# Rotary halves swapped by transfers inside SBUF instead of by matrix products, in a one-layer hybrid attention kernel

## What is computed

```python
def _rope(x, cos, sin):
    x1, x2 = jnp.split(x, 2, axis=-1)
    return jnp.concatenate([x1 * cos - x2 * sin, x2 * cos + x1 * sin], axis=-1)
```

## Time and profile before

| | |
|---|---|
| median of 3 runs | 2755.79 us |
| profiled execution | 2759.88 us |
| its span on the core | 2758.1 us, granted TensorE clock 0.972 |
| TensorE busy | 91% |
| VectorE busy | 63% |
| ScalarE busy | 51% |
| GpSimd busy | 15% |

### The profile page before, as it was taken

How to read it: one execution, slowest core, us unless ns; L and a number is a source line. 1 busy time by engine, 2 the same in 40 slices (tenths; PEclk the granted TensorE clock), 3 DMA queues, 4 the chain that set the end, 5 groups by cost and what they waited for, 6 DMA issues and landing times.

```text
span 2758.1 us, 36858 instructions
## 1 busy us (share of the span) xinstructions
PE 2501.3 (91%) x12861; PEld 2076.0 (75%) x12861; DVE 1749.0 (63%) x3573; ACT 1395.1 (51%) x2817; POOL 410.6 (15%) x397
## 2 busy tenths in 40 slices
PE   5998999998899999998889999999988889888997
PEld 5776888776778888887767788888666677777776
DVE  6467666224667677226777878732578888776652
ACT  5455655343656444224656645523466674545541
POOL 5334253441010000100010010010000000000010
PEclk8999999999999999999999999999999999999999
DMA  5757585794443422565243331146423324211125
GB/s 170 227 170 223 166 274 169 230 295 149 160 159 130 160 93 69 181 223 181 89 158 108 132 120 47 54 163 226 171 96 122 115 87 164 71 54 47 61 89 187
DMA packets 172583, 399.32 MB, mean 145 GB/s; under 512 B 13808, under 2 KB 96752, under 8 KB 162416
## 3 DMA queue, kind: packets, MB, share of 16 engines
q1 hardware_dynamic: 172400, 396.96, 43.2%
HBM read 308.31 MB, written 88.60 MB: 144 GB/s over the span
## 4 chain that ended last, share of the span: by engine, by line
PE 53%; DVE 19%; ACT 16%; issue 10%; DMA 1%; POOL 1%; SPq 0%; DVEq 0%; ACTq 0%; POOLq 0%
PE bank L893 38%; PE TR L789 5%; PE PV L860 5%; ACT signs L1058 4%; ACT prob L1023 3%; ACT prob L1033 3%; ACT ptH L1047 2%; DVE nmx L1427 2%; DVE score L1675 2%; DVE ptL L1458 2%; PE bank L800 2%; PE bank L801 2%; DVE prob L1417 2%; DVE zs L1493 1%; ACT squared L1002 1%
## 5 line engine op out<-in xcount | busy, mean ns | idle before, releaser
L893 PE MATMUL bank<-hH,pairs 128*128 128x512 f32 (+1 forms) x3584 | 1157.6, 393 | 18.1 <-DVE zs L1525 7.6
L893 PEld LDWEIGHTS bank<-hH,pairs 128*128 128x128 f32 x3584 | 678.5, 191 | 156.7 <-issue 18.7
L893 PE MATMUL bank<-hL,pairs 128*128 128x512 f32 (+2 forms) x1792 | 703.4, 393 | 0.0
L1058 ACT ACTIVATE signs<-score,bits 128x384 int8<-128x384 f32 (+7 forms) x256 | 335.8, 1312 | 214.4 <-DVE bits L1558 201.3
L1458 DVE TENSOR_TENSOR ptL<-TR,ptH 128x512 fp32r<-128x512 f32 (+1 forms) x384 | 257.0, 671 | 283.0 <-ACT ptH L1047 280.1
L893 PEld LDWEIGHTS bank<-hL,pairs 128*128 128x128 f32 (+1 forms) x1792 | 343.2, 192 | 64.6
L1047 ACT ACTIVATE ptH<-TR 128x512 fp32r<-128x512 f32 (+1 forms) x384 | 219.5, 576 | 319.5 <-PE TR L789 318.6
L1539 DVE TENSOR_SCALAR_CACHE_REDUCE above<-score,bits 128x256 uint8<-128x256 f32 (+8 forms) x264 | 326.5, 1237 | 9.4
L789 PE MATMUL TR<-identR,prob 128*128 128x128 f32 x1480 | 233.3, 279 | 84.9 <-ACT prob L1033 51.3
L789 PEld LDWEIGHTS TR<-identR,prob 128*128 128x128 f32 x1480 | 180.0, 142 | 158.2 <-ACT prob L1033 65.0
L893 PE MATMUL bank<-ysH,pairs 128*128 128x512 f32 x768 | 257.2, 397 | 10.6 <-issue 5.8
(11 more groups left out here) (215 smaller groups left out, 3648.9 us busy)
## 6 DMA issues: line engine op xcount, KB each, us to landing
pairs<-w_split SPq DMA_DIRECT2D x444, 512.0 KB, 3.5
w_split<-pairs SPq DMA_DIRECT2D x74, 1024.0 KB, 5.0
raw<-in_w_in SPq DMA_DIRECT2D x106, 256.0 KB, 5.6
xs<-in_x SPq DMA_DIRECT2D x4, 2048.0 KB, 9.3
rows<-in_x SPq DMA_DIRECT2D x16, 512.0 KB, 5.0
table<-trig SPq DMA_DIRECT2D x48, 128.0 KB, 3.0
raw<-in_w_branch SPq DMA_DIRECT2D x24, 256.0 KB, 5.8
out<-rows SPq DMA_DIRECT2D x3, 2048.0 KB, 7.5
```

Of the source, the lines that this page charges most:

```text
L893: done = nc.tensor.matmul(PJ[st.u + half * up][0:min(st.width, P), 0:st.n_tok], lhs, rhs[:, row, 0:st.n_tok], start=(n % 12 == 0 and (up o ...
L1058: nc.scalar.activation(signs[:, 0:keys], score[:, tt, 0:keys], ACT.Sign, bias=thr.bitcast(F32)[:, tt:tt + 1], scale=-1.0, accum_out=cnt[:, ...
```

## The change

The halves are swapped by transfers: behind each unit ScalarE issues one transfer per quarter of 32 partitions (four for a unit of 128 channels, two for 64) from `fT` into the new buffer `swapped`. The products L924 and L925, the copy into `fH`, the subtraction into `fL` and `swapR` go. The sign moves into the table: alternate quarters load the sines negated, from a table that is twice as wide. `rotated` adds `swapped` from SBUF instead of `TR` from PSUM. The core of the diff:

```diff
                 if st.role in ROPED:
-                    swaps.append(take("tr"))
-                    steps.append(Step("rope", unit=st, k=st.k, tr=swaps[-1], first=(st is units[0])))
-                    if st.role in ("kv", "kiw"):
-                        f_freed.pop()
-                    f_freed.append(("tr_full", swaps[-1] + 1))
+                    steps.append(Step("rope", unit=st, k=st.k, first=(st is units[0])))
+                    if st.role not in ("kv", "kiw"):
+                        f_freed.append([])
+                    n_swaps[st.k % 2] += 2 if st.role in ("kv", "kiw") else 4
+                    st.swapped = 16 * n_swaps[st.k % 2]
+                    f_freed[-1].append((f"swapped{st.k % 2}", st.swapped))
...
+        def swap_halves(queue, un):
+
+            queue.wait_ge(S["f_sin"], un.k + 1)
+            if un.k >= 2:
+                queue.wait_ge(S["f_sum"], un.k - 1)
+            for q in range(rows_of(un).stop // 32):
+                other = q + 1 - 2 * (q % 2)
+                queue.dma_start(swapped[32 * q:32 * q + 32, un.k % 2, :],
+                                staged(un)[32 * other:32 * other + 32, :]).then_inc(S[f"swapped{un.k % 2}"], 16)
...
-                    sp.wait_ge(S["sin_ready"], 2)
-                    for i, of in enumerate((1, 0)):
-                        sp.dma_start(trig.rearrange("g f n -> (g f) n")[:, i * T:(i + 1) * T], folded[of][:, :]).then_inc(S["tables_out"], 16)
+                    sp.wait_ge(S["sin_ready"], 3)
+                    for i, of in enumerate((folded[1], folded[0], folded[1], turns)):
+                        sp.dma_start(trig.rearrange("g f n -> (g f) n")[:, i * T:(i + 1) * T], of[:, :]).then_inc(S["tables_out"], 16)
...
-                elif st.kind == "rope":
-                    lanes = rows_of(st.unit)
-                    pe.wait_ge(S["tr_free"], st.tr - 1)
-                    pe.wait_ge(S["f_lo"], st.k + 1)
-                    bank = TR[st.tr % 2][lanes, :]
-                    nc.tensor.matmul(bank, swapR[lanes, lanes], fH[lanes, :], start=True, stop=False)
-                    nc.tensor.matmul(bank, swapR[lanes, lanes], fL[lanes, :], start=False, stop=True).then_inc(S["tr_full"], 1)
...
-                    act.wait_ge(S["f_sin"], st.k + 1)
-                    if st.k:
-                        act.wait_ge(S["tr_full"], swaps[st.k - 1] + 1)
-                    nc.scalar.activation(fH[lanes, :], staged(st)[lanes, :], ACT.Copy).then_inc(S["f_hi"], 1)
+                    swap_halves(act, st)
...
+                    act.wait_ge(S["sin_ready"], 2)
+                    nc.scalar.activation(turns[:, :], folded[0][:, :], ACT.Copy, scale=-1.0).then_inc(S["sin_ready"], 1)
...
-                    act.wait_ge(S["tr_free"], st.tr + 1)
+                    act.wait_ge(S["f_sum"], st.k + 1)
...
-                if st.role in ROPED and last == PRODUCTS:
-                    lanes, f = rows_of(st), staged(st)
-                    pool.wait_ge(S["f_hi"], st.k + 1)
-                    nc.gpsimd.tensor_tensor(fL[lanes, :], f[lanes, :], fH[lanes, :].bitcast(F32), ALU.subtract).then_inc(S["f_lo"], 1)
...
-                dve.wait_ge(S["tr_full"], st.tr + 1)
+                dve.wait_ge(S[f"swapped{st.k % 2}"], st.unit.swapped)
                 dve.wait_ge(S["dve_pj"], st.unit.used)
-                TT(turn[lanes, st.k % 4, :], TR[st.tr % 2][lanes, :], turn[lanes, st.k % 4, :], ALU.add).then_inc(S["tr_free"], 1)
+                TT(turn[lanes, st.k % 4, :], swapped[lanes, st.k % 2, :], turn[lanes, st.k % 4, :], ALU.add).then_inc(S["f_sum"], 1)
```

More of the change, by code:

```diff
@@ L73, in __init__ @@
         self.tr, self.p, self.pv, self.before, self.slots, self.behind = tr, p, pv, before, slots, behind
-        self.tiles, self.kept, self.gates, self.stored = tiles, kept, None, None
+        self.tiles, self.kept, self.gates, self.stored, self.swapped = tiles, kept, None, None, None
         self.scale, self.norm, self.woven, self.ring, self.read = scale, norm, woven, ring, read
@@ L86, in order_of_work @@
     count = dict(act_pj=0, dve_pj=0, act_s=0, dve_s=0, pool_x=0)
-    pj_freed, s_freed, x_freed, f_freed, swaps = [], [], [], [], []
+    pj_freed, s_freed, x_freed, f_freed, n_swaps = [], [], [], [], [0, 0]
     last_out, last_gates, places_of = None, [], {}
@@ L179, in turned @@
                 if st.role in ROPED:
-                    steps.append(Step("halve", unit=st, k=st.k, tr=swaps[-1]))
+                    steps.append(Step("halve", unit=st, k=st.k))
         if finishing is not None:
@@ L407, in order_of_work @@
     finish_last(NG - 1)
-    return steps, every, pj_bank, s_bank, s_freed, x_freed, f_freed, swaps
+    return steps, every, pj_bank, s_bank, s_freed, x_freed, f_freed
 def hybrid_block(nc, x, mem, positions, g_in, w_in, attn_sinks, g_mem, w_mem_kv, w_branch, w_out,
                  g_final, out):
-    steps, units, pj_bank, s_bank, s_freed, x_freed, f_freed, swaps = order_of_work()
+    steps, units, pj_bank, s_bank, s_freed, x_freed, f_freed = order_of_work()
     x_v = x[0].rearrange("(g t p) d -> g p t d", t=NT, p=P)
@@ L421, in hybrid_block @@
     mem_scratch = nc.dram_tensor("mem_scratch", (P, 4096), F32, kind="Internal").ap()
-    trig = nc.dram_tensor("trig", (NG, HD // 2, 2 * T), F32, kind="Internal").ap()
+    trig = nc.dram_tensor("trig", (NG, HD // 2, 4 * T), F32, kind="Internal").ap()
     once = sum(st.src == "w_mem_kv" for st in units)
@@ L495, in hybrid_block @@
         fT = sb("fT", [P, 2, T], offset=p_at)
-        fH, fL = (sb(name, [P, T], F32R, p_at + 4096 + i * 2048) for i, name in enumerate(("fH", "fL")))
+        swapped = sb("swapped", [P, 2, T], offset=p_at + 4096)
         turn = sb("turn", [P, 4, T], offset=p_at + 8192)
@@ L523, in hybrid_block @@
         wmask = sb("wmask", [P, 2, 256], F32R)
-        identR, swapR = sb("identR", [P, P], F32R), sb("swapR", [P, P], F32R)
+        identR = sb("identR", [P, P], F32R)
         wi = sb("wi", [P, NT, 4])
@@ L640, in hybrid_block @@
         block = ctx.enter_context(nc.Block())
-        freed_by = {n: S[n] for n in ("act_pj", "dve_pj", "act_s", "dve_s", "p_exp", "pool_x", "tr_full")}
+        freed_by = {n: S[n] for n in ("act_pj", "dve_pj", "act_s", "dve_s", "p_exp", "pool_x", "tr_full", "swapped0", "swapped1")}
         def blocks_of(tile, un):
@@ L663, in gate_of @@
             return kept[:, st.m, :] if st.kept else sg[:, st.x % 2, :]
+        def swap_halves(queue, un):
[6 more added lines that the diff above has]
+                                staged(un)[32 * other:32 * other + 32, :]).then_inc(S[f"swapped{un.k % 2}"], 16)
         def wait_free(eng, ring, index):
             if index >= 2:
-                engine, value = ring[index - 2]
-                eng.wait_ge(freed_by[engine], value)
+                for engine, value in ring[index - 2] if type(ring[index - 2]) is list else [ring[index - 2]]:
+                    eng.wait_ge(freed_by[engine], value)
         def wait_bank(of_kind, index):
@@ L750, in _ @@
                         rows_at = slice(32 * quarter, 32 * quarter + 32)
-                        sp.dma_start(table[rows_at, :, :].rearrange("p a n -> p (a n)"), trig[st.g]).then_inc(S["tables_in"], 16)
+                        sp.dma_start(table[rows_at, :, :].rearrange("p a n -> p (a n)"),
+                                     trig[st.g, :, quarter % 2 * 2 * T:(quarter % 2 + 1) * 2 * T]).then_inc(S["tables_in"], 16)
                 elif st.kind == "unit":
@@ L1282, in _ @@
             pool.wait_ge(S["consts"], 1)
-            link(nc.gpsimd.memset(made[:, :], 0.0))
-            for q in range(4):
-                to, other = made[:, 32 * q:32 * q + 32], 32 * q + (-32 if q % 2 else 32)
-                link(nc.gpsimd.affine_select(out=to, in_=to, compare_op=ALU.not_equal, fill=1.0 if q % 2 else -1.0,
-                                             base=-other, pattern=[[-1, 32]], channel_multiplier=1))
-            link(nc.gpsimd.tensor_copy(swapR[:, :], made[:, :]))
             link(nc.gpsimd.memset(wmask[:, :, :].bitcast(F32), 0.0))
```

7 lines of the change are left out of this document (3 added, 4 removed).

## The result

The changed kernel takes **2782.0 us** (median of 4 runs, 2778.9 to 2784.7), against 2755.6 for the kernel before on the same chip: a ratio of 1.009 (95% interval 1.0074 to 1.0106). It is slower by 26 us by the medians, where the forecast was 27 us faster; the time lies 30 us over the range and close to rival A's 2785. The profiled execution took 2781.2 us, 21.3 us of span more than before.

What follows compares the result with a forecast made beforehand. Pace was set by TensorE in most sparse stages, VectorE in group 3's, and a VectorE-ScalarE ring in window stages. Terms summed to -27.1 us: profiled 2759.9 to 2732.8, median 2729; range 2713 to 2752.

Steps and rivals of the forecast that it cites:

- rival A: Four issues cost ScalarE 3.83 us and it becomes the bound; decides from about 3 us; +29, 2785 us, chance 0.11.
- Step 2: ScalarE drops a 0.63 us copy and issues four transfers for 1.72 us, taken from SyncE's table loads; bounds nothing and 3.83.
- step 3: First stages, groups 1 to 3: fT starts 7.81 us apart for 8.92; 3.1 us gained a stage, 9.2 for three.
- Step 4: Window stages: 2.9 us gained a stage, 8.7 for groups 1 to 3; 2.0 in group 0 (bounds 0 and 6).
- hold-up of 0.76: Window stages: GpSimd's fL delays a small VectorE step by 0.76 us for three q; the change would remove this.
- (a): Window q rounds: issues end at 822.42, signs wanted at 822.37, so ScalarE is 0.05 us late and 0.7 is left.
- (b): Window ak: issues end at 785.2, landing adds 2.2 to 3.0 us; 0.8 us counted of the 1.05 possible.
- Step 1: 104 products removed: 5.5 us gained in group 0's first stage and groups 1 and 2's sparse stages, 0.9 in group 0's sparse.
- Step 5: Sparse stage of group 3, bound by VectorE: two hold-ups by GpSimd go, 1.5 us gained.
- Step 6: Elsewhere: transfers have the next projection, 5.5 us, to land; start costs +0.7; table stores nothing; group 0 may lose 1 us a unit.
- B: Group 0: ScalarE's issues wait for SyncE's on a shared issue path, 0.6 us a unit, +8, 2737 us, chance 0.12.
- C: First stages give nothing as another wait replaces the one for TR, nor does ak: 12 us lost, 2741 us, chance 0.17.

Runs made afterwards that it cites:

- e2: Changed kernel with all transfers still issued, but VectorE adds unswapped fT without waiting for their landing (wrong sum): 2764.2 us, 1.0019 of the kernel before.
- e1: Changed kernel without the swap: no transfers, VectorE adds unswapped fT (wrong sum), products and copies stay out: 2729.4 us, 0.9901 of the kernel before.
- e14: Repeat of e1, the changed kernel without transfers, run beside e13 on the same chip: 2732.2 us, 0.9907 of the kernel before.
- e12: Changed kernel with products in group 0 and for ak, and SyncE issuing the other transfers in groups 1 to 3: 2730.4 us, 0.9904 of the kernel before.
- e9: Changed kernel with the four ak units back on copy, fL and products, ScalarE issuing for the other 48: 2769.8 us, 1.0047 of the kernel before.
- e11: Changed kernel with products in group 0 and SyncE issuing all transfers in groups 1 to 3, ak included: 2733.0 us, 0.9912 of the kernel before.
- e10: Kernel before, all 52 units by products, with only the table of signed sines and a matrix of ones added: 2758.8 us, 1.0003 of the kernel before.
- e7: Changed kernel with SyncE in place of ScalarE issuing the same transfers for all units: 2764.5 us, 1.0033 of the kernel before.
- e3: Changed kernel with one issue a unit for the same bytes, halves copied and not swapped (wrong sum): 2742.9 us, 0.9936 of the kernel before.
- e8: Changed kernel with each transfer cut in two by columns, eight issues a unit on ScalarE, same bytes: 2878.7 us, 1.0437 of the kernel before.
- e13: As e1, but in group 0 VectorE's sum takes its second operand from PSUM (wrong sum): 2731.3 us, 0.9897 of the kernel before.
- e4: Changed kernel with GpSimd in place of ScalarE issuing the same four transfers: 2764.3 us, 1.0018 of the kernel before.

## Why the prediction was wrong, step by step

**Step 2, the price of four issues: right kind, wrong size.** I took 1.72 us from the table loads; it is 2.44. My break-even of 3 us was wrong as well: with 2.44 the kernel is already 26 us slower, and still some 5 us slower where nobody waits for the landing (e2). In the first stage of group 1 the formula of step 3 works with the right price: VectorE's fT starts are 8.62 us apart (663.51, 672.14), against 0.72 + 2.44 + 2.56 + 2.79 = 8.5. The forecast's 7.81 was for 1.72. So -2.7 us for three stages, not -9.2. With SyncE issuing the distance is 7.33, and so it is in e1 without any issue, where the formula would give 6.1: below some 1.2 us for four something else sets the pace, which no run names. e1 has -9.2 for three stages and its repeat e14 -7.6, so the forecast's -9.2 was what issues for nothing give at best.

**Step 4, the window stages: this is the step that failed most, 8.7 us of gain forecast and 10.9 of loss measured.** The hold-up of 0.76 was read rightly: L1539 is at 0.15 us, and e12 gets it whole. The step failed on two terms. *(a) ScalarE would be 0.05 us late.* It is 1 us late at 2.5 us for four, so the 0.7 kept became -0.2 a round. *(b) ak's landing.* I added 2.2 to 3.0 us to the end of the issues and found a gain of 0.8. Measured from the end of the last issue it was 4.7 us in group 1 (793.40 to 798.12), 4.3 and 4.0 in groups 2 and 3; VectorE waited 6.1 to 6.6 us, for 4.4, 4.4 and 3.6 before. The median landing is 3.4 us, up to 6.8, and the earlier trace rows gave the median of transfers issued at other moments. e9 prices this: 11 us in three stages. It is a price of ScalarE's four issues, not of every transfer whose result is asked for at once: in e11 SyncE's landed 1.4 to 2.9 us after the last issue, and did as well as the products.

**Step 1, products removed: the worth was right and was not collected.** In e1 the sparse stages of groups 1 and 2 gain 1.8 us each, my 4 x 0.46, and in e12 a round of the sparse stage of group 1 is 5.44 us where I said 5.5. In the changed kernel group 1 keeps 0.7 and group 2 loses 2.5, since I looked for what TensorE does between two units and not for what stands behind `emptied` on ScalarE: `sides`, for which VectorE waits (2.08 us for 0.74, above). Step 1 names nothing on ScalarE. **Step 5** fails in the same way: -1.5 forecast, +2.1 measured; e12 has -2.9.

**Group 0: not seen.** I gave it -4.7 (steps 1 and 4) and it cost 11 us by the first stage of group 1. What had no slack was the weights' round: over group 0 TensorE waits 15.3 us for GpSimd's splits, where it waited 0.8 before, 6.6 in e1 and 1.5 in e12 with its products. The issues take part (four took 4.12 us at 389.10, beside SyncE's pair at 2.35), and so does the clock above; no run separates the three. Even e1 comes to the first stage of group 1 at +1.

**Step 6**: the start and the tables were right (+0.8 for 0.7; e10 no difference). "A transfer has the whole next projection to land in" held for q rounds in steady state (no waits at 824.56), not for a stage's first units.

**The rivals.** *A* was right in place and sign, and near in time for a wrong reason: 3.83 us was not the common price (two units of 52 reach it), and what made up for it was ak (I had +4, and the landing is about 19 us in e2) and group 0 (I had nothing). *B*'s mechanism is not shown. In group 0 both engines' issues stretch at one moment (4.12 us for four and 2.35 for two, against 2.44 and 1.51). By the Trainium skill (Perfetto Trace Analysis, "DMA Instruction — HWDGE") the recorded time holds the wait for the lock; the rows of that moment agree. But in groups 1 to 3 SyncE issues within 19 rows of four, and 16 of them keep 2.44 to 2.46 us; and in e7, where SyncE alone issues, 7 rows of four are stretched as well, to as much as 3.29, and in the kernel before a single raw load took up to 2.19 (median 0.59). So a second issuer is neither enough nor needed, and what stretches an issue stays open. It is rare: 7 of the 52 units are stretched by 0.3 us or more. *C* gave the first stages nothing; they gave 2.7, and it was the price of the issues that took the rest.

I had put A at 0.11 because of its price, 3.83. The chance should have hung on the point from which it decides, which rested on a ring that I had read with no slack for `sides` and none for the landing.

## What to carry to other kernels

Before an engine is given transfers to issue, read what stands behind the issue on that engine and who waits for it: in groups 1 to 3 the same four issues made ScalarE late for the signs, and SyncE late for nothing. In group 0, where SyncE has the raw weights to load, the same issues from SyncE cost more than from ScalarE. A transfer inside SBUF pays best where a whole step lies between its issue and its use; where the result was asked for at once, ScalarE's four transfers lost to the two products (11 us in three stages, e9), and SyncE's came out even (e11 and e12). Where each way wins in some stages, mix them by a table of stages: it promised 2741 and 2734 us for two mixtures that measured 2743 and 2733.

## What the runs showed of the hardware

- The time of these issues went by neither bytes nor much by the engine: 0.61 us on ScalarE for 32 KB and for 64 KB (0.51 the first of a row), 0.47 for 256 KB of 128 partitions at once, 0.59 on SyncE, 0.50 on GpSimd. The Trainium skill (DMA: Bandwidth & Descriptors, "Rules for kernel authors") says to use one transfer of 128 partitions instead of two to separate halves, and that spreading transfers over issuing engines saves only issue time. e3 against e8 agrees with the first; with the second the runs agree only in part, since the landings differed too (next point).
- A landing was sooner from SyncE (median 2.5 us), whose queue also carries all weights, than from ScalarE's own queue (3.4) or from GpSimd (3.6). Why is open.
- VectorE's sum of two SBUF operands takes up to 1.82 us beside a GpSimd split, and 0.68 with one operand from PSUM. The Trainium skill says (SBUF — State Buffer, "Who interferes with whom") that a VectorE instruction with two SBUF inputs contends with a GpSimd instruction that reads SBUF, and the rows agree. By the traces it cost 3.6 to 4.9 us up to the end of group 0 (e13 against e1 and e14); the times of the whole run don't show it.
- A longer wait of TensorE can lower its clock behind it: 3.65 us at `kiS` in e13, then 0.50 for 6 us; 1.14 us before, and 1.00. No term of the forecast had this. How much it is in all is less sure: summed over stretches of 5 us from 75 us on, PE's busy time x (1 - granted clock) is 52.7 us before and 59.9 in the changed kernel, but 46.7 in e1 and 53.8 in e14, which are one kernel. The mean granted clock is steadier: 0.960 to 0.967 in the four executions of the changed kernel, 0.970 to 0.978 in the 23 of the kernel before that ran beside e1 to e4.
